# Two extra, unused products in every step of a state recurrence on one NeuronCore

## The reference, cut to what matters

```
def step(S, inp):
    r_t, w_t, k_t, v_t, kk_t, a_t = inp
    sa = jnp.einsum('bhij,bhj->bhi', S, -kk_t)
    S = (S * w_t[:, :, None, :]
         + sa[..., None] * (kk_t * a_t)[:, :, None, :]
         + v_t[..., None] * k_t[:, :, None, :])
    y_t = jnp.einsum('bhij,bhj->bhi', S, r_t)
    return S, y_t
```

## Time and profile before

| | before |
|---|---|
| median of 3 runs | 3196.18 us (3189.34 to 3200.56) |
| the profiled execution | 3188.35 us |
| its span, first to last instruction | 3186.4 us |
| mean granted clock | 0.951 |
| PE busy | 2842.3 us (89%) |
| DVE busy | 1918.3 us (60%) |
| ACT busy | 1259.2 us (40%) |

### The profile page before, as it was taken

How to read it: one execution, slowest core, us unless ns; L and a number is a source line. 1 busy time by engine, 2 the same in 40 slices (tenths; PEclk the granted TensorE clock), 3 DMA queues, 4 the chain that set the end, 5 groups by cost and what they waited for, 6 DMA issues and landing times.

```text
span 3186.4 us, 56497 instructions
## 1 busy us (share of the span) xinstructions
PE 2842.3 (89%) x21829; PEld 2368.1 (74%) x21829; DVE 1918.3 (60%) x2115; ACT 1259.2 (40%) x1359; POOL 263.4 (8%) x283
## 2 busy tenths in 40 slices
PE   6998999989899999899159999999999999999970
PEld 5787887978898999744147777777778888888860
DVE  3464646656432211112536767676789999999978
ACT  2302103030122111011125555555567777777751
POOL 1000000000000000000421010101000110001114
PEclk9999999999999999999579999999999999999985
DMA  9000000000011111131237777777789999999998
GB/s 330 22 2 8 14 2 21 2 15 8 2 33 46 40 53 46 49 92 37 85 124 264 260 264 260 263 261 264 259 338 379 376 378 384 383 376 378 382 326 235
DMA packets 149059, 562.46 MB, mean 177 GB/s; under 512 B 19400, under 2 KB 73056, under 8 KB 93650
## 3 DMA queue, kind: packets, MB, share of 16 engines
q1 hardware_dynamic: 124449, 503.18, 43.6%
q0 software_dynamic: 15440, 38.14, 4.1%
q10 hardware_dynamic: 9056, 19.54, 1.6%
HBM read 513.10 MB, written 47.70 MB: 176 GB/s over the span
## 4 chain that ended last, share of the span: by engine, by line
PE 78%; issue 11%; DVE 5%; POOL 3%; DMA 2%; ACT 1%; SPq 0%; DVEq 0%; POOLq 0%; ACTq 0%
PE bank L829 30%; PE bank L1872 12%; PE bank L1873 12%; PE bank L1874 12%; PE bank L1881 5%; PE bank L825 2%; PE bank L1850 2%; POOL rowtok_d L1382 1%; POOL y_got L1446 1%; PE bank L1860 1%; PE bank L1908 1%; DMA y_got<-ys_d,dest 1%; PE bank L1887 1%; DVE P L603 1%; PE bank L880 1%
## 5 line engine op out<-in xcount | busy, mean ns | idle before, releaser
L1709 DVE TENSOR_TENSOR w_lo<-raw_first,w_hi 128x2048 fp32r<-128x2048 f32 x275 | 619.0, 2283 | 76.7 <-ACT w_hi L1487 76.7
L1487 ACT ACTIVATE w_hi<-raw_first 128x2048 fp32r<-128x2048 f32 x276 | 528.2, 1918 | 262.8 <-PE bank L1881 81.9
L1872 PE MATMUL bank<-w_hi,x_hi 128*128 128x512 f32 x1088 | 439.3, 404 | 3.4 <-ACT yo_rows L1529 3.4
L1873 PE MATMUL bank<-w_lo,x_hi 128*128 128x512 f32 x1088 | 426.1, 392 | 0.0
L1874 PE MATMUL bank<-w_hi,x_lo 128*128 128x512 f32 x1088 | 425.6, 391 | 0.0
L1709 DVE TENSOR_TENSOR w_lo<-raw_rest,w_hi 128x2048 fp32r<-128x2048 f32 x136 | 307.6, 2283 | 24.7 <-ACT w_hi L1487 24.7
L1487 ACT ACTIVATE w_hi<-raw_rest 128x2048 fp32r<-128x2048 f32 x136 | 257.3, 1915 | 120.8 <-PE bank L1887 34.9
L829 PE MATMUL bank<-xm_hi,ring_hi 128*128 128x260 f32 x896 | 261.4, 292 | 17.3 <-DVE dz L781 8.2
L829 PE MATMUL bank<-xm_hi,ring_lo 128*128 128x260 f32 x896 | 254.6, 284 | 0.0
L829 PE MATMUL bank<-xm_lo,ring_hi 128*128 128x260 f32 x896 | 254.5, 284 | 0.0
L1872 PEld LDWEIGHTS bank<-w_hi,x_hi 128*128 128x128 f32 x1088 | 206.0, 189 | 58.6 <-issue 19.2
(11 more groups left out here) (347 smaller groups left out, 4684.2 us busy)
## 6 DMA issues: line engine op xcount, KB each, us to landing
raw_first<-in_w_e_up SPq DMA_DIRECT2D x138, 1024.0 KB, 6.4
raw_first<-in_w_e_gate SPq DMA_DIRECT2D x70, 1024.0 KB, 6.6
raw_rest<-in_w_e_gate SPq DMA_DIRECT2D x70, 1024.0 KB, 4.9
raw_first<-in_w_e_down SPq DMA_DIRECT2D x68, 1024.0 KB, 8.8
raw_rest<-in_w_e_down SPq DMA_DIRECT2D x68, 1024.0 KB, 8.2
ring<-in_w_in SPq DMA_DIRECT2D x40, 512.0 KB, 4.0
ys_d<-ar SPq DMA_DIRECT2D x18, 1024.0 KB
ys_d<-y_rows ACTq DMA_DIRECT2D x34, 512.0 KB, 8.8
```

The source lines that it names most:

```text
L1487: nc.scalar.activation(w_hi[:, j % NRING, :, :], raw_piece(j), ACT.Copy).then_inc(hi_done, 1)
L1709: nc.vector.tensor_tensor(w_lo[:, j % NRING, :, :], raw_piece(j), w_hi[:, j % NRING, :, :].bitcast(f32), ALU.subtract).then_inc(lo_done, 1)
L1872: nc.tensor.matmul(ps[:, :], hi, w_hi[:, slot, k, :], start=start and k == 0, stop=False)
L1873: nc.tensor.matmul(ps[:, :], hi, w_lo[:, slot, k, :], start=False, stop=False)
```

## The change

After the mark of each of the nine steps PE makes two further products, one for each head: the same weights, `mxt`, against the 208 columns of `ar` for the chunk. They have the tile shape of the step's own products. They write bank 2, which nobody reads before the products with `x1t` overwrite it. No wait, no mark and no buffer is added or moved.

```
--- before.py
+++ after.py
@@ -968,6 +968,8 @@
                 for h in range(2):
                     ins = mm(bank[6][hp(h), HS * (c % 2):HS * (c % 2 + 1)], mxt[hp(h), c, :], S[hp(h), c, :])
                 pe_j.mark(ins, ('s', c))
+                for h in range(2):
+                    mm(bank[2][hp(h), 0:2 * TP], mxt[hp(h), c, :], ar[hp(h), c, :, :].rearrange("p m t -> p (m t)"))
             dve_j.done(pe, ('nn', 1), j)
             for g in range(2):
                 for c in range(5 * g, 5 * g + 5):
```

## The result

The change makes the kernel faster by half a per cent: median 3178.27 us (3173.28 to 3184.77, 6 runs) against 3196.67 us (3189.34 to 3200.56, now 6 runs), ratio 0.9948 with a 95% interval of 0.993 to 0.9965, that is 11 to 22 us. Run once more beside other kernels it gave 0.9932 (0.9911 to 0.9952), that is 15 to 28 us.

What follows compares the result with a forecast made beforehand. PE was taken to bound the kernel (89% busy, 78% of the chain). Four iterations of 12.97 us make 51.9 us against 65.3, saving 13.4 us: ratio 0.9958, predicted 3183 us, range 3174 to 3202 us.

Steps and rivals of the forecast that it cites:

- The clock stays: In the nine steps: with the pairs PE is busy about 0.77 of each 0.80 us and keeps 2.4 GHz (clock 1.00).
- The sum: First step to end of the `U` products: 12.97 us an iteration, 51.9 us for four against 65.3, saving 13.4 us.
- The price of a pair: PE time of one added pair at full clock: 0.43 us taken, low end 0.37, high end 0.70.
- rival 1: The two products of a pair do not overlap: 0.70 us a pair, saving 11.0 us, 3185 us; chance 0.08.
- Steps 1 to 8 cost nothing: The pair ends at 0.54 us, the next step's weights load at 0.77; PE's wait for DVE hides it, 0.23 us spare.
- Rival 2: The clock falls in the recurrence all the same, nothing comes back: +5.3 us, 3201.5 us; chance 0.18.
- Rival 3: The gain is lost to clock falls in the late stretches: up to 8.4 of 13.4 us, 3191 us; chance 0.09.
- the stretch that I named: The late stretch, from the variance products to the next iteration's first products: 20.3 us with the clock down, 17.5 without.
- Rival 4: The step's mark reaches DVE only after the queued pair: steps grow by it, up to +10.1 us, 3206 us; chance 0.07.
- The whole: Total time: 13.4 us saved, ratio 0.9958 applied to the median 3196.18 us, giving 3182.8 us.

## Why the prediction was right

- *The clock stays.* It did, in four of four iterations in both profiles. This was the weak link, argued from stretches of a like density, and the argument was thinner than it looked. It took PE as busy for 0.77 of each 0.80 us, with under 0.1 us idle; measured are 0.69 us busy and 0.12 us idle, so this sign of the forecast failed. With one head's product, busy 0.65 of 0.80 us at full clock, the clock fell. The argument had nothing in it that puts 0.69 on one side and 0.65 on the other, so that the pair was just enough was in part luck. Why the pair held the clock stays open. That PE is busy in a stretch doesn't tell its clock: the `x1t` products of the kernel before have no idle and ran at 0.50, and so did a stretch busy for 10.00 of 10.00 us (above).
- *The sum.* Predicted 51.9 us for the four recurrences, measured 51.92 and 51.87. Two terms were off and cancelled: the ninth step with its pair was put at 0.70 us and took 0.61 to 0.65 (841.24 to 841.85, 278.14 to 278.79), and the `x1t` products were put at 1.9 and took 1.98. One reading of before was too good: the `U` products were not back at 1.00 in the second iteration (0.81, in 2.35 us); the sum of 65.3 us holds this and is right.
- *The price of a pair.* 0.43 us was taken between 0.37 and 0.70. Behind step 9 it is 0.38 us (51.92 less 50.41, in four), near the low end of 0.37 from the `ar` products, which have the same tile shape, and not the row with the same columns. The two heads overlap, so rival 1 falls, and with it the rule of the Trainium skill on row tiles and one PSUM bank (TensorEngine Tiling (Array Packing), Restrictions and Gotchas) as far as it would slow this pair: 0.55 us for two products against 0.51 for one, both heads in one bank.
- *Steps 1 to 8 cost nothing.* Their period is 0.80 us. The next step's loads stand at 0.78 us (837.12), 0.01 later than forecast, and the pair has ended 0.09 us before. Two pairs used up the cover and cost 0.02 us a step.
- *Rival 2*, the clock falls all the same, did not happen with the change; it is what happened with half of it.
- *Rival 3*, given back later, did happen in part: 5.3 us in the first profile, at the a/w products and not in the stretch that I named, and one such fall in the second. A kernel that gained nothing had the same falls, so the change is not shown to be their cause.
- *Rival 4*, the mark held up by the products behind it, is refuted by DVE's start 0.04 us after the step's own records, and by the step of 0.82 us with eight extra records behind it.
- *The whole.* The medians differ by 18.4 and 23.2 us, against 13.4 predicted. The first interval (11 to 22 us) holds the prediction, the second (15 to 28 us) doesn't. The stretch from the first step to the last variance products gained 11.1 to 16.6 us by the four profiles. What lies behind this stretch, which the change doesn't touch, took 2323.5 and 2326.4 us in the two profiles of before and 2327.6 and 2323.3 in the two of after, so the single profile differences (4.0 us of span in the first pair) say little. Whether the surplus over 13.4 is more than this scatter stays open.

## What to carry to other kernels

A ping-pong of two engines can cost PE twice: in the waits, and in the dense work right behind them, which here ran at half clock. Read the granted clock by windows over the stretch behind the waits, and not only over the waits. Unused products in the waits can pay if they end before the next real one. Which are enough, only the changed kernel's own windows tell: here half the columns, or one head's product of the two, gave nothing. Here the last waits before the dense work were the place: in each iteration, four pairs there gave the whole gain, four in the first waits none, and nine behind the waits none. And compare the busy share of two kernels only at the same clock, because a slower clock makes the same work look busier.

## What was not expected

With one 64*64 product of 208 columns in each step the clock fell to 0.50, and with two side by side, in nearly the same time (0.51 and 0.55 us), it stayed at 1.00, as it did with one 128*128 product of 0.62 us. And the clock could stay down under products that left PE no idle time: just behind the levels it read 0.50 over 10 us, in the kernel with four more waits filled and in the second profile of the kernel before.
